# A half block of S runs its products with U's high part first, behind a wait of their own

## The reference

```
u = jnp.take(expert_u, it, axis=0)
h = jnp.einsum('chkd,cd->chk', u, xt).astype(jnp.float32)
a = gt * jax.nn.gelu(h, approximate=False)
vv = jnp.take(expert_v, it, axis=0)
return jnp.einsum('chk,chkd->cd', a.astype(x.dtype), vv)
```

## Time and profile before

| | |
|---|---|
| median of 3 runs | 2421.46 us (2420.43 to 2421.61) |
| the profiled execution | 2421.28 us, its span 2419.5 us |
| busy: PE, PEld, DVE, ACT, POOL | 96%, 87%, 70%, 46%, 27% of the span |
| mean granted TensorE clock | 0.986 of 2.4 GHz |
| L671, products of split units | first 1008.2 us, last 1689.9 us |

### The profile page before, as it was taken

The page is one execution under the profiler, slowest core; times in us unless marked ns, Lnnn a source line. Parts: engine busy times, 40 slices in busy tenths (PEclk is TensorE's granted clock), DMA queues, the critical chain, the costliest instruction groups (busy, mean ns, idle before and its releaser), DMA issues.

```text
span 2419.5 us, 45242 instructions
## 1 busy us (share of the span) xinstructions
PE 2333.2 (96%) x14770; PEld 2106.2 (87%) x14770; DVE 1684.4 (70%) x2628; ACT 1106.1 (46%) x1716; POOL 649.6 (27%) x425
## 2 busy tenths in 40 slices
PE   7999999999899979999999999999999999999996
PEld 7988799878897779999999999999788888888885
DVE  4444556655644555799999999998577767777556
ACT  3444455543433333345544454454444444444442
POOL 0000000000201020778877786565100000000100
PEclk9999999999899989999999999999999999999998
DMA  8788544565354545677878787777888878887763
GB/s 316 250 278 265 188 140 148 162 220 192 134 178 122 193 133 140 149 188 187 189 187 187 186 188 189 186 189 198 282 293 286 282 250 283 285 289 273 242 220 122
DMA packets 333365, 507.60 MB, mean 210 GB/s; under 512 B 69072, under 2 KB 216784, under 8 KB 325744
## 3 DMA queue, kind: packets, MB, share of 16 engines
q1 hardware_dynamic: 285856, 443.79, 58.8%
q0 software_dynamic: 46736, 62.17, 11.0%
q10 hardware_dynamic: 704, 0.75, 0.1%
HBM read 485.33 MB, written 21.23 MB: 209 GB/s over the span
## 4 chain that ended last, share of the span: by engine, by line
PE 83%; DVE 7%; DMA 4%; issue 3%; SPq 1%; ACT 1%; DVEq 0%; POOL 0%; ACTq 0%; POOLq 0%
PE ps L703 28%; PE ps L460 18%; PE ps L671 17%; PE ps L466 15%; DVE u_lo L1430 3%; DMA u_raw<-in_peer_u_dram 3%; PE ps L660 1%; DVE u_turned L1424 1%; SPq L383 1%; DMA temps<-gates_scratch 1%; PE ps L608 1%; PE ps L626 1%; DMA weight_ring<-in_w_in_dram 0%; DVE split_ring L1217 0%; PE ps L644 0%
## 5 line engine op out<-in xcount | busy, mean ns | idle before, releaser
L671 PE MATMUL ps<-parts,u_hi 128*128 128x240 f32 x3904 | 670.2, 277 | 7.0 <-DVE u_lo L1430 4.6
L1217 DVE TENSOR_TENSOR split_ring<-weight_ring,split_ring 128x1024 fp32r<-128x1024 f32 x288 | 353.2, 1233 | 365.9 <-ACT split_ring L788 364.8
L671 PEld LDWEIGHTS ps<-parts,u_hi 128*128 128x128 f32 x3904 | 586.6, 189 | 18.3 <-DVE u_lo L1430 14.5
L1160 POOL DMA_INDIRECT gates_scratch<-sb_gains x256 | 520.1, 2032 | 170.5 <-issue 99.1
L703 PE MATMUL ps<-parts,temp_parts 128*128 128x512 f32 x2304 | 545.8, 390 | 5.5 <-DVE parts L1566 5.5
L671 PE MATMUL ps<-parts,u_lo 128*128 128x240 f32 x1952 | 536.2, 275 | 0.0
L703 PEld LDWEIGHTS ps<-parts,temp_parts 128*128 128x128 f32 x2304 | 434.0, 188 | 96.7 <-DVE parts L1566 6.3
L788 ACT ACTIVATE split_ring<-weight_ring 128x1024 fp32r<-128x1024 f32 x288 | 302.9, 1059 | 368.5 <-PE ps L460 226.1
L460 PE MATMUL ps<-split_ring,parts 128*128 128x512 f32 x1920 | 439.9, 391 | 5.6 <-DVE parts L1333 3.9
L460 PEld LDWEIGHTS ps<-split_ring,parts 128*128 128x128 f32 x1920 | 360.8, 188 | 80.9 <-DVE split_ring L1217 4.1
L973 ACT ACTIVATE u_hi<-u_turned 128x1024 fp32r<-128x1024 f32 x244 | 258.9, 1061 | 342.8 <-DVE u_turned L1424 341.4
(11 more groups left out here) (222 smaller groups left out, 1414.1 us busy)
## 6 DMA issues: line engine op xcount, KB each, us to landing
u_raw<-in_peer_u_dram SPq DMA_DIRECT2D x1024, 128.0 KB
region<-in_peer_v_dram SPq DMA_DIRECT2D x256, 512.0 KB, 4.5
weight_ring<-in_w_in_dram SPq DMA_DIRECT2D x96, 512.0 KB, 5.0
weight_ring<-in_w_mkv_dram SPq DMA_DIRECT2D x64, 512.0 KB, 3.8
gates_scratch<-temps POOLq DMA_DIRECT2D x16, 1024.0 KB, 7.4
weight_ring<-in_w_o_dram SPq DMA_DIRECT2D x32, 512.0 KB, 3.7
weight_ring<-in_w_mq_dram SPq DMA_DIRECT2D x32, 512.0 KB, 3.7
weight_ring<-in_w_mo_dram SPq DMA_DIRECT2D x32, 512.0 KB, 3.6
```

The costliest lines, as they stand in the source:

```text
L671: m = nc.tensor.matmul(ps[:, b, 0:ET], u[:, c], x[kk][:, 0:ET], start=kk == 0 and n == 0, stop=kk == KB - 1 and n == 2)
L1160: pool.indirect_dma_start(gates_by_one, bass.IndirectOffsetOnAxis(ap=idx_all[:, j:j + 1], axis=0), gate_all[:, j:j + 1], None, compute_op= ...
L1217: nc.vector.tensor_tensor(w_lo[j % SPLIT], raw[j % RAW], w_hi[j % SPLIT].bitcast(F32), ALU.subtract).then_inc(lo_ready, 1)
```

## The change

In `split_unit` the wait for `u_lo_ready` ahead of all 24 products becomes two waits. PE first waits for `u_hi_ready` of the unit, runs the 16 products with `u_hi` (chunk by chunk, with the tokens' high part and their rest), then waits for `u_lo_ready` and runs the 8 products with `u_lo`. The accumulation starts with the first of the 16 and stops with the last of the 8, which counts `u_used` as before. Nothing else is edited.

```
             def split_unit(i, h, slot, b):
 
+                def half_sums(u, halves, done):
+                    for k in range(KB // 2):
+                        kk = h * (KB // 2) + k
+                        for n in halves:
+                            m = nc.tensor.matmul(ps[:, b, 0:ET], u[:, k * P:(k + 1) * P], x2T[n][kk][:, 0:ET],
+                                                 start=not done and kk == 0 and n == 0, stop=done and kk == KB - 1)
+                    return m
+
+                pe.wait_ge(u_hi_ready, i * 2 + (h + 1 - NATIVE))
+                half_sums(u_hi[slot], (0, 1), False)
                 pe.wait_ge(u_lo_ready, i * 2 + (h + 1 - NATIVE))
-                for k in range(KB // 2):
-                    kk = h * (KB // 2) + k
-                    c = slice(k * P, (k + 1) * P)
-                    for n, (u, x) in enumerate(((u_hi[slot], x2T[0]), (u_hi[slot], x2T[1]), (u_lo[slot], x2T[0]))):
-                        m = nc.tensor.matmul(ps[:, b, 0:ET], u[:, c], x[kk][:, 0:ET], start=kk == 0 and n == 0,
-                                             stop=kk == KB - 1 and n == 2)
-                m.then_inc(u_used, 1)
+                half_sums(u_lo[slot], (0,), True).then_inc(u_used, 1)
```

## The result

The kernel after takes 2396.22 us in the median of 5 runs (2392.49 to 2397.55), the kernel before 2421.61 us in 5 (2420.43 to 2423.48): a ratio of 0.9896, 95% interval 0.9885 to 0.9907. It is 25.4 us faster. The changed line L671 is now L670, L1424 is L1428, and L1430 is L1434.

A forecast was written before the change was run, and what follows sets the result against it. PE, 96% busy, was taken as the bound, with gaps from late L1430 subtractions in search passes. 2421.46 - 21.4 (stalls covered) + 0 (added wait) = 2400.1, stated as 2400.0 us; range 2397.5 to 2407 us for 8 in 10.

The forecast's parts named there:

- Two engines with too little slack between them; the gaps end with L1430: Split units, twelve search passes: PE and its weight loads waited 19.1 us for L1430, DVE 20.3 us for PE.
- The greatest lateness, 1.3 us, is below 1.8 us.: Split units: DVE falls at most 1.3 us behind PE, so the 1.8 us of 16 u_hi products cover every stall.
- The list of steps: Eight DVE transpose starts of one pass, 1120.61 to 1140.72, compared with PE's 2.70 us per unit to get DVE's lateness.
- Twelve times 48.61 is 583.3, so the searches cost PE 605.93 - 583.3 = 22.6 us.: Twelve search passes priced against 18 units without searches (48.61 us): at most 22.6 us to gain.
- DVE's floor lies between 48.47 and 48.8 us: DVE's least time per pass, from busy time and waits; gives a gain of 20.3 to 22.6 us, middle 21.4.
- The added wait at 0: One more semaphore wait on PE in each of 244 units costs 0, with 4.9 us as the other bound.
- The rule of the Trainium skill: A wait in mid unit could expose a weight load on PE; by this rule some 2446 us instead of 2400.
- V stays behind PE; the scatter-adds do not bind: Start of V stage: POOL's scatters leave 15 us of slack and move forward with DVE, so V still follows PE.
- 1: Rival: a satisfied wait in mid unit costs 0.02 us, giving back 4.9 us; 2405 us, chance 0.1.
- 2: Rival: DVE sets the pace, its pass not shrinking below 49.5 us; gain 12 us, 2409 us, chance 0.05.
- 3: Rival: the stall only moves to PE's second wait and nothing is won; 2421 us, chance 0.03.
- 4: Rival: slower, the wait cuts the run-ahead of weight loads, up to one load per unit; 2446 us, chance 0.03.

The follow-up runs named there:

- e1: Kernel before with all 24 products in the new order behind the old single wait for u_lo_ready; 2422.25 us (10 runs), ratio 1.0002 to the kernel before.
- e3: Kernel before edited to the new order, with only eight u_hi products ahead of the wait for u_lo_ready and sixteen behind; 2400.44 us (one run).
- e6: Kernel after with one further comparison over 512 columns on DVE in each pass, results unused; 2392.11 us (one run), stage of split units 658.2 us.
- e7: Kernel after with two further comparisons over 512 columns on DVE in each pass, results unused; 2406.94 us (one run), stage of split units 665.5 us.
- e5: Kernel after with seven further, already satisfied waits for u_hi_ready in each unit; 2395.49 us (4 runs), ratio 0.9888 to the kernel before.

## Why the prediction was right in kind and short in size

- **Two engines with too little slack between them; the gaps end with L1430.** Right. With the order alone nothing changes (e1); with the cover all 19.1 us of waits are gone.
- **"The greatest lateness, 1.3 us, is below 1.8 us."** Right, and nearly in size: 1.45 us measured, a margin of 0.48 us left. The list of steps ended one too early. The steps did not become shorter behind 1140.72; the next was 2.86 us, against PE's 2.70, and brings the sum to 1.37 us. The rest is PE's pace, which is 48.38 / 18 = 2.69 us. The eight products of e3 and the extra work of e6 go beyond the cover and stall. The row that the list lacks:

```profile
1143.58 1.25 DVE L1424 STREAM_TRANSPOSE u_turned<-u_raw 128x1024 f32<-128x1024 f32 x1
```

- **"Twelve times 48.61 is 583.3, so the searches cost PE 605.93 - 583.3 = 22.6 us."** This is the step that failed. I took the stretch without searches, where PE was busy throughout, as PE's own floor. It was not: 48.61 us still held 0.23 us of late starts at nine block borders, each 0.02 to 0.03 us and so without an idle row, from the same cause that the change removes. The floor in these kernels is 48.38 us (in e7 alone the units behind the loop came 0.01 us closer, which stays open). That is 3.1 us in all, 2.5 us in the passes and 0.6 us in the 28 units behind them (75.8 us before, 75.2 after), which I gave no place in sum or range.
- **"DVE's floor lies between 48.47 and 48.8 us", of which I took the middle, 1.2 us less gain.** Wrong at both ends: the floor is 47.9 to 48.0 us (e6, e7). Busy time is not the least time, since the same work is 48.47 us of it in a pass before and 47.92 after, and a pass less its visible waits holds the same reserve. With 21.4 + 1.2 + 3.1 = 25.7 us the sum is the measured one.
- **The added wait at 0, with 4.9 us as the other bound.** The value was right (e5: nothing over 1708 waits), the bound was not needed. It came from the 0.02 us of block borders, which were not a wait's price. One misreading thus cut the gain and also stretched the range to the wrong side.
- **The rule of the Trainium skill.** "TensorE: Matmul & The Clock Gate", Step-by-step, has weight loads pulled ahead of products in flight, and I took from it that a wait in mid unit might expose them. The trace does not bear out the loss: 0.0 us idle ahead of all 5856 weight loads with 488 waits, and e5 the same with 1708 more.
- **V stays behind PE; the scatter-adds do not bind.** Right: V kept its length within 0.5 us (729.5 and 730.0 us).
- **Rivals.** 1 is out by e5, 2 by passes of 48.40 us (580.78 / 12), 3 and 4 by the result. "DVE sets the pace" comes true, nearly, only with work added (e6, e7).

## What to carry to other kernels

A consumer that needs its operands in parts should wait for each part where it is first read. What that is worth can be read from the producer's steps: add up how late it runs against the consumer's pace; stalls end when the cover exceeds the greatest lateness, provided that the producer has time to catch up again before the next run of long steps (0.4 to 0.5 us a pass here), and the last part of the cover is worth little (1.4 us for the last four products here, 6.3 us for the first two).

A stretch in which the bounding engine shows 100% busy is not yet its floor. If its producer finishes only 0.15 us ahead there too, compare the spacing at unit borders with that inside a unit before taking it as the least time.

Before a small gain is read off whole runs, look at the granted clock of the stretches that the change does not touch. Here it moved the time by 4 us, as much as the forecast missed.

## What was unexpected of the hardware

A product that starts 0.15 us after the end of what it waited for has been followed late, by about 0.02 us, without any idle time in the view (0.36 us for three steps in place of 0.34). Where the product really had to wait, those behind it came another 0.1 us late (e6). Block borders show the 0.02 us, with a lead of 0.15 us by the rows, and borders inside a block, with 0.16, don't; what lies behind it I did not test. Satisfied semaphore waits on PE cost nothing that can be seen even at eight in 16 products. And the first 300 us of the program took up to 5.6 us more or less from run to run in identical code, with the granted clock behind the same short pauses at its lower level in some executions and not in others. That is more than most of the effects tested here, while the later stage, at a clock of 1.00, repeated within 0.1 us.
